# A fourth product block in every other gate/up chunk, and a later load of two normalisation rows, in a hybrid decoder layer

## The reference

```python
h = layer_norm(ALPHA*h + 0.5*swiglu(h, w_gate1, w_up1, w_down1), ln1_g, ln1_b)
mix = hybrid_mixer(h, ...)       # SSD branch and window attention
h = layer_norm(ALPHA*h + mix, ln2_g, ln2_b)
h = layer_norm(ALPHA*h + 0.5*swiglu(h, w_gate2, w_up2, w_down2), ln3_g, ln3_b)

def swiglu(x, w_gate, w_up, w_down):
    return (jax.nn.silu(x @ w_gate) * (x @ w_up)) @ w_down
```

## Time and profile before

| | |
|---|---|
| median of 3 runs | 2651.43 us (2650.16 to 2652.53) |
| the profiled execution | 2652.16 us |
| its span, first to last instruction | 2650.5 us |
| TensorE busy | 2625.1 us, 99% of the span |
| VectorE busy | 2081.4 us, 79% |
| ScalarE busy | 1379.9 us, 52% |
| GpSimd busy | 129.6 us, 5% |
| mean granted TensorE clock | 0.997 |

### The profile page before, as it was taken

How to read it: one execution, slowest core, us unless ns; L and a number is a source line. 1 busy time by engine, 2 the same in 40 slices (tenths; PEclk the granted TensorE clock), 3 DMA queues, 4 the chain that set the end, 5 groups by cost and what they waited for, 6 DMA issues and landing times.

```text
span 2650.5 us, 35957 instructions
## 1 busy us (share of the span) xinstructions
PE 2625.1 (99%) x12519; PEld 2180.2 (82%) x12519; DVE 2081.4 (79%) x2372; ACT 1379.9 (52%) x1663; POOL 129.6 (5%) x170
## 2 busy tenths in 40 slices
PE   9999999999999999999999999999999999999997
PEld 7888888888887788888888888878888888888886
DVE  6989989798666665677777765887788989897986
ACT  4555555455444454556655554454465555554553
POOL 1000000000000000211111100000000000000000
PEclk9999999999999999999999999999999999999999
DMA  7666666766655546655655566656666666667564
GB/s 222 195 198 206 191 204 194 231 202 199 196 178 146 158 149 194 206 182 181 181 178 176 177 180 177 219 191 209 213 208 201 190 210 189 203 196 260 190 212 169
DMA packets 286471, 514.03 MB, mean 194 GB/s; under 512 B 19664, under 2 KB 53120, under 8 KB 284320
## 3 DMA queue, kind: packets, MB, share of 16 engines
q1 hardware_dynamic: 279824, 485.03, 58.7%
q0 software_dynamic: 4880, 25.36, 2.6%
q10 hardware_dynamic: 1664, 2.26, 0.2%
HBM read 506.23 MB, written 6.36 MB: 193 GB/s over the span
## 4 chain that ended last, share of the span: by engine, by line
PE 93%; DVE 4%; ACT 1%; issue 1%; DMA 0%; POOLq 0%; ACTq 0%; POOL 0%; SPq 0%; DVEq 0%
PE acc L827 11%; PE acc L829 11%; PE acc L828 11%; PE acc L931 5%; PE acc L933 5%; PE acc L932 5%; PE spare L931 5%; PE spare L933 5%; PE spare L932 5%; PE acc L913 4%; PE acc L915 4%; PE acc L914 4%; PE spare L914 3%; PE spare L913 3%; PE spare L915 3%; PE spare L796 2%
## 5 line engine op out<-in xcount | busy, mean ns | idle before, releaser
L1854 DVE TENSOR_TENSOR w_lo<-land,w_hi 128x1024 fp32r<-128x1024 f32 (+1 forms) x956 | 1151.0, 1222 | 413.8 <-ACT w_hi L1396 405.2
L1396 ACT ACTIVATE w_hi<-land 128x1024 fp32r<-128x1024 f32 (+1 forms) x956 | 966.6, 1026 | 900.6 <-DVE land L2081 283.2
L827 PE MATMUL acc<-w_hi,a_hi 128*128 128x512 f32 (+1 forms) x1168 | 444.2, 380 | 1.0 <-DVE w_lo L1854 0.8
L829 PE MATMUL acc<-w_hi,a_lo 128*128 128x512 f32 (+1 forms) x1168 | 428.9, 367 | 0.0
L828 PE MATMUL acc<-w_lo,a_hi 128*128 128x512 f32 (+1 forms) x1168 | 427.6, 366 | 0.0
L827 PEld LDWEIGHTS acc<-w_hi,a_hi 128*128 128x128 f32 x1168 | 220.4, 189 | 45.0 <-issue 10.1
L829 PEld LDWEIGHTS acc<-w_hi,a_lo 128*128 128x128 f32 x1168 | 220.2, 189 | 37.4
L828 PEld LDWEIGHTS acc<-w_lo,a_hi 128*128 128x128 f32 x1168 | 220.7, 189 | 36.9 <-issue 3.8
L913 PE MATMUL acc<-w_hi,a_hi 128*128 128x512 f32 x512 | 201.7, 394 | 0.7 <-DVE w_lo L1854 0.7
L915 PE MATMUL acc<-w_hi,a_lo 128*128 128x512 f32 x512 | 199.6, 390 | 0.0
L914 PE MATMUL acc<-w_lo,a_hi 128*128 128x512 f32 x512 | 199.4, 390 | 0.0
(11 more groups left out here) (454 smaller groups left out, 4364.5 us busy)
## 6 DMA issues: line engine op xcount, KB each, us to landing
land<-w_in SPq DMA_DIRECT2D x232, 512.0 KB, 3.8
land<-ffn_w_gate SPq DMA_DIRECT2D x176, 512.0 KB, 4.0
land<-ffn_w_up SPq DMA_DIRECT2D x176, 512.0 KB, 4.2
land<-ffn_w_down SPq DMA_DIRECT2D x176, 512.0 KB, 4.7
land<-w_ssd_o SPq DMA_DIRECT2D x64, 512.0 KB, 4.5
land<-w_in SPq DMA_DIRECT2D x132, 128.0 KB, 2.3
land<-w_attn_o SPq DMA_DIRECT2D x32, 512.0 KB, 4.1
land<-w_out SPq DMA_DIRECT2D x32, 512.0 KB, 4.7
```

The lines of the kernel that those rows point to most:

```text
L827: pe.matmul(to, rows_hi, hi, start=first, stop=False)
L829: mm = pe.matmul(to, rows_lo, hi, start=False, stop=last)
L1396: act.activation(w_hi[:, l % SPLIT, 0:deep, 0:width], land[:, l % LAND, 0:deep, 0:width], ACT.Copy).then_inc(high, 1)
L1854: dve.tensor_tensor(w_lo[:, l % SPLIT, 0:deep, 0:width], land[:, l % LAND, 0:deep, 0:width], w_hi[:, l % SPLIT, 0:deep, 0:width].bitcast(F ...
```

## The change

Four things change.

1. `SEVEN` becomes (2, 4, 5, 6), and there are three kinds of chunks: "four" (chunks 1, 3, 5, 7; pairs 2, 4, 5, 6), "three" (chunks 2, 4, 6, 8; pairs 2, 4, 6) and "last" (chunks 9 and 10; pairs 2, 4, 6). Each feed-forward part has four blocks more.
2. A second set of the weight sums, `t_hi_two` and `t_lo_two`, is used in turn with the first in chunks 1 to 8; it lies where the hidden rows of later chunks will be. ScalarE then waits for TensorE's block before the last (`t_used` less `free`).
3. In the chunks of four, `copy_one` and `collect` stand at slab 2 instead of slab 1. A fourth set of mixed rows is made in chunk 0, so that the sets stand at slabs 8, 10, 12 and 14.
4. GpSimd waits for slab 27 of the second half of `wso`, the second slab of its last block, before it loads `ln1_g` and `ln1_b`.

```diff
-SEVEN = (2, 4, 6)
+SEVEN = (2, 4, 5, 6)
+UP_SEVEN = {"four": (2, 4, 5, 6), "three": (2, 4, 6), "last": (2, 4, 6)}
+UP_T_SET = {"four": (0, 1, 0, 1), "three": (0, 1, 0), "last": (0, 0, 0)}
+UP_T_FREE = {"four": (0, 1, 1, 1), "three": (1, 1, 1), "last": (0, 0, 0)}
+LOOPED = 8
+COLLECT_AT, SUM_AT = {"four": 2, "three": 1, "last": 1}, {"four": 3, "three": 3, "last": 3}
...
+        t_sets = [(t_hi, t_lo), (placed("t_hi_two", [P, 3, W], F32R, 32 * K), placed("t_lo_two", [P, 3, W], F32R, 76 * K))]
...
             pool.wait_ge(mix_out, MIXED)
+            pool.wait_ge(used, slab_no("wso", 1, 27) + 1)
             load_rows(rows, ln1_g, ln1_b, rows_in)
...
-            def t_high_part(n):
+            def t_high_part(n, t_set=0, free=0):
 
                 act.wait_ge(sums, n * 3 + 3)
-                if not is_zero(n):
-                    act.wait_ge(t_used, n)
-                act.activation(t_hi[:, :, :], t_sums, ACT.Copy).then_inc(t_high, 1)
...
+                if not (isinstance(n, int) and n <= free):
+                    act.wait_ge(t_used, n - free)
+                act.activation(t_sets[t_set][0][:, :, :], t_sums, ACT.Copy).then_inc(t_high, 1)
...
-                    elif l == 1:
+                    elif l == COLLECT_AT[kind]:
                         collect(f, i - 1, 1 - odd)
-                    elif l == 3:
+                    elif l == SUM_AT[kind]:
                         sum_chunk(f, i - 1, 1 - odd)
-                    elif l == 4:
+                    elif l == SUM_AT[kind] + 1:
                         product_summed(f, i - 1)
...
-                for i in range(1, ALONE + 1):
-                    up_seven(f, i, i % 2)
-                with dve.Fori(1, 1 + (NC_S - ALONE) // 2) as m:
+                for k, kind in enumerate(("four", "three")):
+                    up_seven(f, 1 + k, 1 - k, kind, 0)
+                with dve.Fori(1, LOOPED // 2) as m:
                     ch.enter(m, 1, SEVEN_LINKS)
-                    for k in range(2):
-                        up_seven(f, m * 2 + (ALONE - 1 + k), (ALONE + 1 + k) % 2)
-                    ch.leave(1 + (NC_S - ALONE) // 2)
+                    for k, kind in enumerate(("four", "three")):
+                        up_seven(f, m * 2 + (1 + k), 1 - k, kind, m)
+                    ch.leave(LOOPED // 2)
+                for i in range(LOOPED + 1, NC_S + 1):
+                    up_seven(f, i, i % 2, "last", i)
```

More of the change, by code:

```diff
@@ L96 @@
               for j in range(2)]
-UP_BLOCKS = NC_S * len(SEVEN)
+TWO_CHUNKS = len(UP_SEVEN["four"]) + len(UP_SEVEN["three"])
+UP_BLOCKS = LOOPED // 2 * TWO_CHUNKS + (NC_S - LOOPED) * len(UP_SEVEN["last"])
 ALL_BLOCKS = UP_BLOCKS + sum(DOWN_BLOCKS)
@@ L222, in summed_no, with seven_block, chunk_ahead @@
     return i + ((f - 1) * NC_S - 1)
-def seven_block(f, i, b):
-    return i * len(SEVEN) + ((f - 1) * ALL_BLOCKS - len(SEVEN)) + SEVEN.index(b)
+def seven_block(f, kind, m, b):
+    at = (f - 1) * ALL_BLOCKS + UP_SEVEN[kind].index(b)
+    if kind == "last":
+        return at + LOOPED // 2 * TWO_CHUNKS + (m - LOOPED - 1) * len(UP_SEVEN["last"])
+    return m * TWO_CHUNKS + (at + (len(UP_SEVEN["four"]) if kind == "three" else 0))
+def chunk_ahead(kind, m):
+    if kind == "last" and m > LOOPED + 1:
+        return "last", m - 1
+    return ("three", LOOPED // 2 - 1 if kind == "last" else m - 1) if kind != "three" else ("four", m)
 def down_block(f, j, q):
@@ L933, in three, with seven_products @@
                 return pe.matmul(to, rows[1], block[0], start=False, stop=last)
-            def seven_products(n, slab_at, l, rows_of, mixed, own, aux, first, last, turned=None):
+            def seven_products(n, slab_at, l, rows_of, mixed, own, aux, first, last, turned=None, t_set=0):
                 def block(l, k):
@@ L1070, in up_seven @@
                         pe.wait_ge(mix_out, (f - 1) * MIXED + len(SEVEN))
[L1071 to L1072 removed]
+                    if b in UP_SEVEN[kind]:
+                        up_seven_block(f, i, b, own, aux, kind, at)
                     else:
@@ L1563, in down @@
                         if j == 0 and l == 1:
-                            copy_one(f, NC_S, NC_S % 2)
+                            copy_one(f, NC_S % 2, "last", NC_S)
                         if j == 0 and l == 4:
```

88 lines of the change are left out of this document (49 added, 39 removed).

## The result

The changed kernel takes **2657.7 us** (median of 17 runs, 2654.7 to 2661.7), the kernel before 2652.2 (17 runs, 2650.2 to 2655.5). The ratio is 1.0021, 95% interval 1.0014 to 1.0028: slower by about 5.5 us. The prediction said 2647.9, with a range to 2652.5, and gave "slower" 7 in 100. It was wrong.

What follows compares the result with a forecast made beforehand. TensorE's matmuls were taken to set the time in gate and up, with VectorE close behind. -5.4 + 3.0 + 2.5 - 3.7 = -3.6 us on 2652.16 gave 2648.6, or 2647.9 in terms of the median; range 2644.0 to 2652.5.

Steps and rivals of the forecast that it cites:

- The matmuls, -5.4: Gate and up, both feed-forward parts: four pairs each go from 24 to 21 matmuls at 0.2267 us, -5.4 us.
- The added work in chunks of four, +3.0: Gate and up: TensorE waits 0.5 us at slab 12 of chunks 3, 5, 7, twice; +3.0 us, bounds 0 and 7.
- a pitch of 1.67 us: Gate and up: VectorE's time for a low part, within the 4.26 us that one more block costs it.
- With one set, about 1 us.: Chunks of four: ScalarE's high part of pair 6 would wait about 1 us for TensorE; second set counted at 0.
- The later collecting, 0: Chunks of four: `collect` behind slab 1 fills VectorE's idle time while `copy_one` waits for TensorE; 0.
- The fourth mixed set, +2.5 and 0: Chunk 0: TensorE waits about 1.7 us at slab 9, 0.8 at slab 10; +2.5 us first part, 0 second.
- The rows, -3.7: wso: moving the load removes a wait and low clock costing 3.67 us, free at its new place; bounds 0 and -3.7.
- VectorE has only one slab per 2.7 us to split: Rows' new place: VectorE's light work there, with no block sums near, supported putting the load at no cost.
- The reload of the earlier trace: Nearest case for the rows' new place: 2 MB reload at 1845.95, with one TensorE wait of 0.21 us beside it.
- VectorE keeps up: Rival: no waits in chunks of four, 2644.9 us; slab 9 of chunk 0 in time, 2645.4; both 2642.4; together 0.25.
- The load as dear: Rival: load costs as much at its new place, or slabs land later in chunks of four; 2651.6 us, chance 0.15.
- Short waits halve the clock: Rival: waits at slab 12 of chunks 3, 5, 7 and slab 9 of chunk 0 cost 11.8 us more; 2659.7, chance 0.07.

Runs made afterwards that it cites:

- e3: Changed kernel with three blocks in every chunk (fourth mixed set and two sets of sums kept) and rows loaded at the old place; 2653.5 us, one execution.
- e10: e5 with e8's edit, and four blocks in chunk 1 alone of each feed-forward part; 2646.8 us against 2652.4 for the kernel before, ratio 0.9980.
- e6: Changed kernel with one set of block sums in place of two; 2674.7 us, one execution.
- e7: Changed kernel with the collecting at slab 1 instead of slab 2 in chunks of four; 2656.7 us, one execution.
- e4: Changed kernel with VectorE's angles in chunk 0 cut into five pieces instead of one stretch before slab 9; 2654.5 us against 2652.4 for the kernel before.
- e1: Kernel before with only the two parameter rows loaded later, behind slab 27 of wso's second half; 2650.9 us against 2652.4, ratio 0.9994.
- e11: Changed kernel with only ScalarE's three small loads moved behind slab 7 of keys and values; 2653.3 us against 2652.4 for the kernel before, ratio 1.0004.
- e9: e5 with e8's edit, and the third sum of every gate and up block on GpSimd; 2675.3 us against 2652.4 for the kernel before, ratio 1.0089.
- e5: e4 with ScalarE's three small loads moved behind slab 7 of keys and values; 2650.8 us against 2652.4 for the kernel before, ratio 0.9995.
- e2: Changed kernel without the later load of the rows; 2659.8 us against 2652.4 for the kernel before, ratio 1.0028.
- e8: Kernel before with the two rows loaded apart, behind slabs 1 and 27 of wso's second half; 2649.3 us against 2652.4, ratio 0.9987.

## Why the prediction was wrong, point by point

Forecast and profile lie 7.8 us apart (-3.6 and +4.2). Three steps make nearly all of it: the added work in chunks of four was sized at 3.0 and cost 6.8, the rows at their new place were put at no cost and took 1.6, and ScalarE's small transfers behind gate and up, which no term held, took 2.0.

- **The matmuls, -5.4.** Right: 24 fewer, each 0.23 us of TensorE.
- **The added work in chunks of four, +3.0.** This step failed by its size. Chunks 3, 5 and 7 lose 1.0 us each in the first part, 3.0 together. In the second part the four chunks of four are +0.87 over before; with 4 x 0.68 for the matmuls they lose 3.6. Chunk 1 of the first part, where 0 was forecast, loses 0.68 - 0.51 = 0.2 without a listed wait, in distances of 0.24 to 0.29 around slab 12. In all 6.8, at the upper bound of 7. The mechanism, VectorE late at slab 12, was as laid out, place and all (the rows for it were of chunk 7, not 5; all odd chunks read the same). What failed is the sum of pitches: a pitch of 1.67 us was read where another instruction follows a low part, and used where a sum follows it (1.79 and 1.95). And the wait was priced as its length alone; behind it the next matmul came 0.34 us on in place of 0.23, and a later one 0.29.
- **"With one set, about 1 us."** The second set belonged in the sum at 0 and cost 0 (e3, e10). The argument for it looked at the wrong handover; without it the change would have cost some 17 us more (e6, one execution).
- **The later collecting, 0.** Right (e7).
- **The fourth mixed set, +2.5 and 0.** Right to 0.04 us, with waits of 1.31 and 0.63 where 1.7 and 0.8 were forecast. The cause given, the angles just before it, is shown by e4.
- **The rows, -3.7.** Half right. The gain in wso was 3.6 to 3.7 us in every run with the new place, against a profiled execution whose clock fell there. The step that failed is "VectorE has only one slab per 2.7 us to split": it also has 7.06 us of merging between the third and the fourth slab, and behind it no lead. So the load cost 1.6 us there (1.1 in e1, 1.8 in e4, 0 in e7). The reload of the earlier trace rows, taken as the nearest case, waits for that merging and is issued behind it, at 1845.95, so it could not show this. The bound "0 to -3.7" did hold it.
- **Keys and values, not in the sum.** +2.0 us in the profile; with the small transfers moved, the timed runs give back 4.4 (e11). No step of the prediction asked what else ScalarE's queue does behind gate and up.
- **Sum.** -5.4 + 6.8 + 2.5 - 2.1 + 2.0 = 3.8, and 0.3 at the end, against 4.2 by the profiles. The timed runs add about 1.3 to that, as the profiled execution lies 1.2 us below their median; where the others lost it is not shown.
- **The rivals.** "VectorE keeps up" was wrong in all chunks of four in the loop. "The load as dear" was right by some 40%. "Short waits halve the clock", the only way to slower that was priced, did not happen in the changed kernel's profile: behind the waits at 41.43, 45.08, 348.90, 738.97 and 1849.55 the clock reads 1.00. It is no empty rival, though: at slab 12 itself the clock fell in e9, behind waits of 2.24 and 2.25 us in chunks 3, 5 and 7, and in keys and values in e4, e6 and e7. The Trainium skill's rule on frequent micro-idles (TensorE: Matmul & The Clock Gate, section "A second HAM failure mode: psum-queue depth-cycling"), which the prediction weighed, is not borne out by the change: with a wait in three chunks of each part, the mean clock over both stretches of gate and up reads 1.00.
- **The range.** The prediction's own upper bounds, -5.4 + 7 + 4.2 - 0, give +5.8, 2657.2 in terms of the median. The range ended at 2652.5, as if only one term could come out badly, and the chance of 0.07 for slower goes with that. With two terms near their bounds and a stall at a third place the time came out above it.

What stays open: why the issue of the first small transfer takes 2.4 to 3.7 us in programs with chunks of four in the loop. It goes with the program and with that moment (e5, e11), while e3, whose program differs from e2's in the fourth blocks alone, has 0.40. GpSimd's transfers of the kept rows were under way in both, and SyncE issued nothing in these microseconds. Nothing tried here separates them further.

## What to carry to other kernels

When an engine is the critical one's supplier and has no lead, price its added work by the pitch of exactly the pairs of instructions that will follow each other; then add what the waiting engine loses behind the wait. Before adding work at one place, look for bulk work of the same engine just ahead of it that can be spread (the angles), and put the extra block where the supplier has lead (chunk 1) and not where it has none. Look at every transfer issued by a compute engine near a tight place: its issue occupies that engine, and a transfer of 2 MB in one go can be better cut in two at two places (e8). For each place ask what longer piece of work the supplier has between two slabs, and whether it is just in time behind it.
